# Experts of a mixture layer: picking the rows of two pairs with one set of 256-column products

## The reference, cut to what matters

```python
N_GROUPS, EXPERTS_PER_GROUP, N_EXPERTS, TOP_K, D_EXPERT = 4, 8, 32, 2, 512
# router: one group by softmax, then the two best of its eight experts, with gates
# every token goes through its two experts:
(jax.nn.silu(xb @ w1[e]) * (xb @ w3[e])) @ w2[e]      # w1, w3: 1024 x 512, w2: 512 x 1024
# results weighted by the gates are added up per token
x = x + gate2 * y_moe
return _rmsnorm(x, final_norm_w)
```

## Time and profile before

| what | us |
|---|---|
| median of 3 runs (1502.05 to 1504.66) | 1503.75 |
| the profiled execution | 1503.93 |
| its span, from first to last instruction | 1502.1 |
| mean granted TensorE clock | 0.977 |
| expert stage in the trace | about 243 to 707 |

### The profile page before, as it was taken

The page is one execution under the profiler, slowest core; times in us unless marked ns, Lnnn a source line. Parts: engine busy times, 40 slices in busy tenths (PEclk is TensorE's granted clock), DMA queues, the critical chain, the costliest instruction groups (busy, mean ns, idle before and its releaser), DMA issues.

```text
span 1502.1 us, 16975 instructions
## 1 busy us (share of the span) xinstructions
PE 1378.2 (92%) x6322; PEld 720.0 (48%) x6322; DVE 789.1 (53%) x1912; ACT 292.8 (19%) x714; POOL 340.8 (23%) x321
## 2 busy tenths in 40 slices
PE   6999999999999999999999999997997787778787
PEld 4886665444444444443566665553543332323333
DVE  2257665322332332333426887757676766767555
ACT  1435312000000000001334333221212121212112
POOL 0005303000000000000000345444544443444451
PEclk9999999999999999999999999999999999998899
DMA  9743788999999999999342699999999999999997
GB/s 381 299 158 130 282 329 309 426 426 425 426 425 426 427 426 427 425 426 425 146 175 106 267 391 396 421 421 421 421 421 421 421 422 421 422 421 422 420 422 306
DMA packets 64579, 551.35 MB, mean 367 GB/s; under 512 B 9168, under 2 KB 9440, under 8 KB 11760
## 3 DMA queue, kind: packets, MB, share of 16 engines
q1 hardware_dynamic: 26080, 278.06, 44.8%
q0 software_dynamic: 38416, 272.17, 44.0%
HBM read 549.16 MB, written 1.05 MB: 366 GB/s over the span
## 4 chain that ended last, share of the span: by engine, by line
PE 63%; DMA 31%; issue 2%; ACT 1%; DVE 1%; POOL 1%; SPq 0%; POOLq 0%; DVEq 0%
DMA ring<-peer_uv_d,work 19%; PE ps L2086 13%; PE ps L1986 11%; PE ps L2138 7%; PE ps L1327 6%; DMA work<-peer_uv_d,work 4%; PE ps L1814 4%; PE ps L1321 4%; PE ps L1775 3%; PE ps L2096 3%; DMA ring<-w_ada_d 2%; PE ps L1643 2%; DMA ring<-expert_w_d 2%; DMA work<-expert_w_d 2%; DMA consts_sb<-peer_uv_d,work 2%
## 5 line engine op out<-in xcount | busy, mean ns | idle before, releaser
L1986 PE MATMUL ps<-ring,work 128*128 128x512 f32 x686 | 338.9, 636 | 78.0 <-ACT work L1258 77.1
L3355 DVE CUSTOM_DVE_ANT_0 ring<-ring,work 128x1024 f32<-128x1024 f32 x172 | 211.4, 1230 | 137.8 <-DMA ring<-peer_uv_d,work 136.1
L1986 PEld LDWEIGHTS ps<-ring,work 128*128 128x128 f32 x686 | 134.2, 202 | 260.0 <-issue 151.6
L2314 POOL DMA_INDIRECT ring<-peer_uv_d,work x170 | 187.3, 1102 | 240.6 <-PE ps L1986 215.6
L2086 PE MATMUL ps<-ring,work 128*64 128x512 f32 x768 | 168.1, 593 | 1.4 <-DMA ring<-expert_w_d 0.9
L1258 ACT ACTIVATE work<-consts_sb,work 128x128 f32<-128x128 f32 x256 | 85.3, 392 | 285.1 <-DVE work L3364 277.2
L2086 PEld LDWEIGHTS ps<-ring,work 128*64 128x64 f32 x768 | 56.6, 137 | 109.7 <-issue 109.7
L1327 PE MATMUL ps<-ring,hT 128*128 128x512 f32 (+1 forms) x256 | 105.7, 567 | 0.1
L2896 DVE TENSOR_TENSOR work<-work,ps 128x512 f32<-128x512 f32 x16 | 11.0, 687 | 177.2 <-PE ps L2086 177.2
L2288 POOL DMA_DIRECT2D mod<-subkeys_d x1 | 0.5, 548 | 456.3 <-DVEq L2963 456.3
L1106 ACT ACTIVATE work<-ps 128x512 f32<-128x512 f32 x16 | 9.6, 597 | 430.7 <-PE ps L2086 430.7
(11 more groups left out here) (486 smaller groups left out, 1748.3 us busy)
## 6 DMA issues: line engine op xcount, KB each, us to landing
ring<-expert_w_d SPq DMA_DIRECT2D x72, 2048.0 KB, 19.3
work<-expert_w_d SPq DMA_DIRECT2D x36, 1024.0 KB, 18.7
ring<-w_ada_d SPq DMA_DIRECT2D x12, 2048.0 KB, 9.3
ring<-w_in_d SPq DMA_DIRECT2D x11, 2048.0 KB, 22.7
consts_sb<-expert_w_d SPq DMA_DIRECT2D x12, 1024.0 KB, 19.7
ring<-w_out_d SPq DMA_DIRECT2D x4, 2048.0 KB, 8.3
ring<-peer_w_query_d SPq DMA_DIRECT2D x4, 2048.0 KB, 7.9
ring<-w_in_d SPq DMA_DIRECT2D x4, 1024.0 KB, 30.0
```

Source lines behind the costliest of these rows:

```text
L1986: last = pe.matmul(ps[V_BANK[t] + n][:, :], diag[:, i % 4, :], v_row(i)[:, n * 512:(n + 1) * 512], start=(i % (16 * PH) == 0), stop=(i == ...
L2314: pool.indirect_dma_start(out=uv_rows(i), out_offset=None, in_=io["peer_uv"], in_offset=bass.IndirectOffsetOnAxis(ap=idx[:, s, k:k + 1], a ...
L3355: dve.tensor_tensor_reduce(out=u_row(i), in0=u_row(i), in1=h_tok[:, i // (16 * PH), :], scale=1.0, scalar=0.0, op0=ALU.mult, op1=ALU.add, ...
```

## The change

Pair 0 and pair 15 are still picked alone; the pairs 1 and 2, 3 and 4, ..., 13 and 14 are picked together (`gathered_with`), by 16 products of 256 columns in four banks, during the even pair ahead of them. The tiles pm and xeT hold two pairs and have moved, with pg and pgT, to other addresses. An odd pair picks nothing: between its layer "b" and the transposes it spreads two of the four results of the pair before, the other two come after the transposes, and its w3 tiles are given free by the first transpose. VectorE follows the same order; it makes the masks of two pairs in an even pair. The number of places stays eight; place and turn of a tile are worked out by two functions with the same values as before. GpSimd zeroes qz after the experts instead of before (its old address is now pm's). The waits for the two biases become one semaphore, so that the first waits for both. The dense branch has other addresses for its tiles.

```diff
@@ -254,16 +254,34 @@
         return self.turn[i - self.banks] if i >= self.banks else None
+def gathered_with(p):
+    return 2 if 0 < p < PAIRS - 1 else 1
+def tile_place(n):
+    return n % PLACES
+def tile_turn(n):
+    return sum(tile_place(m) == tile_place(n) for m in range(n + 1))
 def expert_jobs():
     jobs = [("g00", "D"), ("g01", "D")]
     for p in range(PAIRS - 1):
         jobs += [(f"a{p}", "A"), (f"b{p}", "D")]
-        jobs += [(f"g{p + 1}0", "D"), (f"g{p + 1}1", "D")]
-        jobs.append((f"at{p}", "D"))
-        if p:
-            jobs += [(f"sc{p - 1}{n}", "D") for n in range(4)]
+        if p % 2 == 0:
+            jobs += [(f"g{p + 1}{i}", "D") for i in range(2 * gathered_with(p + 1))]
+            jobs.append((f"at{p}", "D"))
+            jobs += [(f"sc{p - 1}{n}", "D") for n in range(4 if p else 0)]
+        else:
+            jobs += [(f"sc{p - 1}0", "D"), (f"sc{p - 1}1", "D"), (f"at{p}", "D")]
+            jobs += [(f"sc{p - 1}2", "D"), (f"sc{p - 1}3", "D")]
         jobs.append((f"pt{p}", "D"))
...
@@ -474,17 +492,18 @@
         acc = W(2048, TT, D)
-        xeT = W(4096, KC, P)
-        pm = W(5120, TT, P)
-        pg = W(5376, 2, TT, P)
-        pgT = W(5888, TT, P)
+        xeT = W(4096, KC, 2 * P).rearrange("p k (j n) -> p k j n", j=2)
+        pm = W(11776, TT, 2 * P)
+        pg = W(12288, 2 * TT, P).rearrange("p (j t) n -> p j t n", j=2)
+        pgT = W(12800, TT, P)
         sil = W(6144, D_EXP)
         act_p = W(6656, D_EXP)
         actT = W(7168, 4, P)
         y_sb = W(9984, D)
         sil_d = W(4096, 4, T)
         act_d = W(6144, 4, T)
-        acc_s = mod[:, 1:3, :]
+        acc_s = W(0, TT, D)
+        hT_d = [W(5120, 4, T), mod[:, 2, :].rearrange("p (k n) -> p k n", k=4)]
         beside = [[W(2048, 2048), W(13312, 2048)], [consts[:, C_LINC:C_LINC + 2048], W(7680, 2048)]]
...
@@ -1766,14 +1785,16 @@
             def gathered(p):
-                pe.wait_ge(p_ready, p + 1)
-                for g in range(2):
+                pairs = gathered_with(p)
+                width, per = pairs * P, 4 // pairs
+                pe.wait_ge(p_ready, p + pairs)
+                for g in range(2 * pairs):
                     b = fbank(f"g{p}{g}")
-                    for c in range(4):
-                        k = 4 * g + c
+                    for c in range(per):
+                        k = per * g + c
                         for t in range(TT):
-                            last = pe.matmul(b[:, c * P:(c + 1) * P], h_tok[:, t, k * P:(k + 1) * P],
-                                             pm[:, t, :], start=(t == 0), stop=(t == TT - 1))
+                            last = pe.matmul(b[:, c * width:(c + 1) * width], h_tok[:, t, k * P:(k + 1) * P],
+                                             pm[:, t, 0:width], start=(t == 0), stop=(t == TT - 1))
                             if p and k == 0 and t == 0:
...
@@ -2079,11 +2100,13 @@
                     wt = [expert_tile(p, l + u) for u in range(2)]
+                    j = (p - 1) % 2 if gathered_with(p) == 2 else 0
+                    per = 4 // gathered_with(p)
                     for k in range(KC):
-                        if k % 4 == 0:
-                            taken(f"g{p}{k // 4}")
+                        if k % per == 0:
+                            taken(f"g{p - j}{k // per}")
                         for u in range(2):
-                            last = pe.matmul(b[u * CAP:(u + 1) * CAP, :], xeT[:, k, u * CAP:(u + 1) * CAP], wt[u](k),
+                            last = pe.matmul(b[u * CAP:(u + 1) * CAP, :], xeT[:, k, j, u * CAP:(u + 1) * CAP], wt[u](k),
                                              start=(k == 0), stop=(k == KC - 1), skip_group_check=True)
...
@@ -2112,22 +2135,23 @@
                     first_layer(p, "b", 2)
-                    if p < PAIRS - 1:
+                    if p % 2 == 0:
                         gathered(p + 1)
+                    elif p < PAIRS - 1:
+                        scattered(p - 1, 0)
+                        scattered(p - 1, 1)
                     else:
                         scattered(p - 1, 2)
                     b = fbank(f"at{p}")
                     taken(f"b{p}")
                     for c in range(4):
                         last = pe.transpose(b[:, c * P:(c + 1) * P], act_p[:, c * P:(c + 1) * P], ident)
-                        if c == 0 and p == PAIRS - 1:
+                        if c == 0 and p % 2:
                             last.then_inc(w_used, 2)
                     last.then_inc(f_done, 1)
                     if p:
-                        for i in range(4 if p < PAIRS - 1 else 0):
+                        for i in (3,) if p == PAIRS - 1 else (2, 3) if p % 2 else range(4):
                             scattered(p - 1, i)
-                        if p == PAIRS - 1:
-                            scattered(p - 1, 3)
                     turned_places(p)
...
@@ -2276,8 +2303,6 @@
             pool.dma_start(k_nw, io["moba_k_norm_w"].to_broadcast([P, AD])).then_inc(b2_small, 16)
-            for t in range(TT):
-                pool.memset(qz[t], 0.0).then_inc(qz_zero, 1)
             pool.wait_ge(nw_used, 1)
...
@@ -2287,6 +2312,8 @@
             pool.dma_start(mod[:, 0, :], io["norm2_w"].to_broadcast([P, D])).then_inc(in_nw3, 16)
+            for t in range(TT):
+                pool.memset(qz[t], 0.0).then_inc(qz_zero, 1)
             pool.wait_ge(nw_used, 2)
...
@@ -2548,7 +2575,7 @@
                 post(na_sc)
-            dve.wait_ge(in_bias, 16)
+            dve.wait_ge(in_bias_mod, 32)
             window_scores(0)
...
@@ -2818,7 +2845,8 @@
                         e = 2 * p + u
-                        dve.tensor_scalar(pm[:, t, u * CAP:(u + 1) * CAP], io64, rk[:, t, e:e + 1], None,
+                        at = (p - 1) % 2 * P * (gathered_with(p) - 1) + u * CAP
+                        dve.tensor_scalar(pm[:, t, at:at + CAP], io64, rk[:, t, e:e + 1], None,
                                           ALU.is_equal).then_inc(sel_n, 1)
...
@@ -2870,9 +2898,12 @@
                 def rows_in(p):
-                    for g in range(2):
+                    pairs = gathered_with(p)
+                    per = 4 // pairs
+                    for g in range(2 * pairs):
                         b = fjob(f"g{p}{g}")
-                        ftook(dve.tensor_copy(xeT[:, 4 * g:4 * g + 4, :], b[:, :].rearrange("p (c n) -> p c n", c=4)))
+                        ftook(dve.tensor_copy(xeT[:, per * g:per * (g + 1), 0:pairs, :],
+                                              b[:, :].rearrange("p (c j n) -> p c j n", c=per, j=pairs)))
                 def added(p, pieces=range(4)):
...
@@ -2887,21 +2918,24 @@
                     if p < PAIRS - 1:
-                        places(p + 1)
+                        for later in range(p + 1, p + 1 + gathered_with(p + 1)) if p % 2 == 0 else ():
+                            places(later)
                         weighted_places(p + 1)
                     else:
                         added(p - 1, (0, 1))
                     b = fjob(f"b{p}")
                     dve.wait_ge(f_a, FAST.taken(f"a{p}"))
                     ftook(dve.tensor_tensor(act_p, sil, b[:, :], ALU.mult))
-                    if p < PAIRS - 1:
+                    if p % 2 == 0:
                         rows_in(p + 1)
+                    elif p < PAIRS - 1:
+                        added(p - 1, (0, 1))
                     else:
                         added(p - 1, (2,))
                     b = fjob(f"at{p}")
                     ftook(dve.tensor_copy(actT.rearrange("p a b -> p (a b)"), b[:, :]))
                     if p:
-                        added(p - 1, range(4) if p < PAIRS - 1 else (3,))
+                        added(p - 1, (3,) if p == PAIRS - 1 else (2, 3) if p % 2 else range(4))
                     b = fjob(f"pt{p}")
...
```

More of the change, by code:

```diff
@@ L864, in _ @@
                 for q in range(24):
+                    n = PLACES + q
                     sp.wait_ge(w_used, i * 24 + (q + 3))
-                    expert_tile(i * 8 + (2 * ((8 + q) // 6) + q % 2), (8 + q) % 6, q % PLACES)
-            for q in range(72, N_MOE - PLACES):
-                sp.wait_ge(w_used, q + 3)
-                expert_tile(2 * ((8 + q) // 6) + q % 2, (8 + q) % 6, q % PLACES)
+                    expert_tile(i * 8 + (2 * (n // 6) + n % 2), n % 6, q % PLACES)
+            for n in range(PLACES + 72, N_MOE):
+                sp.wait_ge(w_used, n - PLACES + 3)
+                expert_tile(2 * (n // 6) + n % 2, n % 6, tile_place(n))
             for i in range(len(tiles2)):
@@ L1759, in expert_tile @@
             def expert_tile(p, l):
-                place, turn = (6 * p + l) % PLACES, (6 * p + l) // PLACES + 1
+                place, turn = tile_place(6 * p + l), tile_turn(6 * p + l)
                 if place < RING:
@@ L2166, in _, with full_pairs, tile_of @@
                 pe.wait_ge(full_copied, 2 * TT)
-                with pe.Fori(0, PAIRS // 4) as i:
```

(29 more changed lines are left out.)

17 lines of the change are left out of this document (8 added, 9 removed).

## The result

| kernel | median us (runs) | profiled execution, span |
|---|---|---|
| before | 1503.38 (22) | 1503.93, 1502.1 |
| after | 1506.20 (22; 1504.65 to 1508.25) | 1507.81, 1505.9 |

The ratio is 1.0018 [1.0012, 1.0024]: 2.7 us (1.8 to 3.6) slower, where 1.8 us was forecast. The range held it. One run of before, 1536.02 us, was in a slower state and is left out of the ratio. The profiled execution of after is one of its slower ones, so I read stages in it, not its total.

What follows compares the result with a forecast made beforehand. The prediction took the weight-tile transfers to bound the expert stage, with TensorE arriving at the same moment. From the profiled 1503.93 us (median 1503.75), +1.8 for one hole and 0 for the rest gave 1505.6 us, range 1501.0 to 1508.0.

Steps and rivals of the forecast that it cites:

- What bounds the stage: Expert stage: it ends when the weight-tile transfers end, 29.5 us a pair against 28.61 us of TensorE.
- The saving: Picking on TensorE: 0.35 us less for each of seven couples, 2.45 us in all, worth nothing by itself.
- The late release at pair 1: Pair 1's first products, which free pair 0's output tiles, come 3.33 us later, from 273.91 to 277.2.
- The size of the hole: Gap in the tile transfers near 278 us: 3.33 - 1.5 = 1.8 us, bounds 0.8 and 2.8.
- the slack of 1.5 us: The tile issue at 275.1 could come as late as 276.6 without breaking the stream of transfers.
- the bound of 2.8: Upper bound in us of the gap, if the landing at 279.6 was late through one DMA engine of 16.
- the rival without slack: At the issue of 275.1 the whole 3.33 us slip is lost, 1507.1 us; chance 0.18 together with two holes.
- The page's fixed part: About 2.0 us fixed per DMA by the skill page, against 2.9 from the rows; gives a 0.9 us hole.
- Later places: Tile issues after the first gap, in pair 1 and at pair 3 (slack 1.2 to 2.2 us): no second gap.
- TensorE's waits: Waits for expert tiles grow from 2 us to some 6; waits of 1 to 2 us leave the clock at 1.00.
- The end: End of the expert stage: last tile landing and TensorE's arrival each 1.8 us later, last landing near 697.2.
- Small edits: Merged bias wait, moved memsets, final-norm weights fetched 1 us earlier: worth nothing, covered by idle time or the natural hole.

Runs made afterwards that it cites:

- twice_pair8: The kernel before the change with the picking of pair 8's rows done twice, in pair 7; 1504.54 us, ratio 1.0005.
- twice_pair1: The kernel before the change with the picking of pair 1's rows done twice, in pair 0; 1506.31 us, ratio 1.0020.
- pick_after_output: The changed kernel with pair 0's double picking put behind pair 0's output layer; 1505.84 us, ratio 1.0013 to the kernel before.
- single_start: The changed kernel with pairs 1 and 2 picked alone, couples beginning with 3 and 4; 1505.18 us, ratio 1.0007 to the kernel before.
- small_edits: The kernel before the change with only the merged bias semaphore and the later memsets; 1503.92 us, ratio 1.0005.

## Why the prediction was right, and where it was off

- **What bounds the stage: right.** The transfers do. TensorE had 1.6 us less to do and the stage grew; twice_pair8 shows the other side, 3.6 us more work for 0.9.
- **The saving: nearly.** 0.35 us for each couple was forecast, 0.23 came (57.22 - 56.99), and it was hidden. The picking itself takes the 7.01 us of the earlier trace rows; what is missing is the first two spreads of an odd pair, 1.82 us (291.86 to 293.68) where 1.72 was reckoned.
- **The late release at pair 1: right, and shown alone** by twice_pair1. Shift 3.33 us, as forecast.
- **The size of the hole: 1.8 forecast, 2.55 measured.** The step that was mis-sized is the slack of 1.5 us, read from one execution. There the tile issued at 262.8 landed at 279.6, a microsecond late; my sum leaned on that microsecond, though the bound of 2.8 named it. In after the forerunner was 0.4 us less late against the stage's start, so the lead was 0.74 and not 4.44 - 3.33 = 1.11. The restart took 8.2 us and not 7.8, another 0.4. With 1.8 these are the 2.55, so that of a shift of 3.33 only 0.8 us was covered: halfway between the forecast and the rival without slack. The slack of one execution was taken for that of all; 4.44 and 4.00 us of lead at the same issue in before and twice_pair8 show how it moves.
- **The page's fixed part: it didn't decide.** The 2.0 us that the prediction quotes from the Trainium skill ("DMA: Bandwidth & Descriptors", Anatomy of one DMA) stand there for transfers that GpSimd issues; these are SyncE's. The restarts here leave 2.9 to 3.7 us beyond the tile, and the hole of 0.9 us by the page did not come.
- **Later places: right for after, and only because of the hole.** At pair 3 the lead is 342.3 - 336.2 = 6.1 us. Without the hole it is 2.8 in pick_after_output, where stalls of TensorE in pair 0 delay pair 3 by 1.1 us on top, and 3.3 in single_start: about the edge. I had counted the hole into that slack and hadn't asked what the place would be like without it.
- **TensorE's waits: right in sum, wrong in form.** Six microseconds were forecast. By the pairs' distances 6.7 went (4.46 + 0.19 + 2.07 over an unstalled pair), where before lost 2.6; 4.4 of them are waits and some 1.7 the half clock. "Waits of 1 to 2 us did not lower it" said more than the earlier trace rows shows, a single wait of 1.07; and the surplus of two pairs comes as one wait.
- **The end: right in kind, and the number by luck.** Last landing 697.6 for 697.2, but 0.8 us of that is the later start of the stage. Within the stage the last landing came 1.3 us later and TensorE's arrival 2.4, where I had 1.8 for both. Both fell together in before because a tile there landed 1.1 us late at 675.7, behind TensorE's last wait; in after no tile does, and TensorE comes 1.2 us behind the last landing. The end hangs on the landing that pair 14 waits for, not on the last one.
- **VectorE: right.** Its copies of the turned activations, in pair 0 and in pair 1, and the stall of 0.72 us ahead of 271.11:

```profile
269.77 0.69 DVE L2905 COPY work<-ps 128x512 f32<-128x512 f32 x1 [1.03 <-PE ps L1796]
270.38 0.68 DVE L2936 COPY work<-ps 128x512 f32<-128x512 f32 x1
...
294.49 0.68 DVE L2936 COPY work<-ps 128x512 f32<-128x512 f32 x1
```

  The second ends at 295.17, 1.0 us before the output layer of pair 1 begins (0.9 forecast).
- **Small edits: right**, by the starts of the stage in all traces and by GpSimd's own row: the memsets stand ahead of 23.27 us of idle time.

```profile
713.04 1.02 POOL L2316 MEMSET work<- 128x512 f32 x2
737.34 0.53 POOL L2318 DMA_DIRECT2D nw<-mix_scale_d  x1 [23.27 <-DVEq L3260]
```

**What stays open.** The 2.3 to 2.6 us of pick_after_output are only in part accounted for: its stage is 1.3 to 1.4 us longer and its stream 1.1 to 1.2, of which the two thin places are 0.2 to 0.5. Why the tile issued at 293.1 and 295.2 is a microsecond late both times isn't shown. Landings that are 0.5 to 1.9 us late occur in every execution, before too, at changing places, and make the stage differ by about a microsecond. Which executions lose time to the clock can't be read from their times alone.

## What to carry to other kernels

Where a bounded number of buffers feeds a stream of transfers, look at each early release by its lead, the time from its issue to its forerunner's landing, and ask for each what remains when work is moved ahead of it; take the latest harmless issue from how long a restart takes on a dry queue, and don't count on a late landing of one execution. Read an engine's busy time over the stage that the change touches: over the whole span it fell by 3.8 us here, none of it in that stage. A saving on the engine that isn't the slower one turns into waiting; if the edit also bunches the waits, the clock can take as much as the edit gave (1.7 against 1.6 us here). When one thin place is mended, the next one of the same kind has to be read again, since the hole had been its cover.

## What the runs showed that I had not expected

The profiled execution of small_edits was 3.5 us longer than the median, and its stage was not. On VectorE one operation of 128x256, begun at 119.66, took 4.74 us instead of 0.4 (5.04 us for two, before 0.71). GpSimd had begun a 128x2048 operation 0.23 us earlier, and the two end 0.3 us apart. At 140.75 it happened again, with an operation of 4.63 us begun 0.03 us behind GpSimd's next one. First VectorE and GpSimd in small_edits, then in before:

```profile
119.36 5.04 DVE L2508 TENSOR_TENSOR ring<-ring,consts_sb 128x256 f32<-128x256 f32 x2
...
119.43 7.19 POOL L2227 TENSOR_TENSOR ring<-ring 128x2048 f32<-128x2048 f32 x2 [2.21 <-ACT ring L1001]
...
140.48 4.90 DVE L2556 TENSOR_SCALAR work<-work,small 128x256 f32<-128x256 f32 x2
140.72 4.51 POOL L2227 TENSOR_TENSOR ring<-ring 128x2048 f32<-128x2048 f32 x1 [7.14 <-ACT ring L1001]
```
```profile
119.70 0.71 DVE L2509 TENSOR_TENSOR ring<-ring,consts_sb 128x256 f32<-128x256 f32 x2
...
120.27 6.99 POOL L2228 TENSOR_TENSOR ring<-ring 128x2048 f32<-128x2048 f32 x2 [2.72 <-ACT ring L1002]
```

In before GpSimd begins 0.14 us before VectorE's pair of operations ends, and nothing is held. So it is in the twelve other traces: the second of VectorE's pair begins 0.06 to 0.68 us ahead of GpSimd's operation (in twice_pair8 0.01 us behind it) and takes 0.41 us. What counts seems to be whether GpSimd is already under way. The stage of small_edits then started 3.9 us later than that of before (251.77 against 247.89). Some runs of before itself, 1506.9 to 1509.3 us where its median is 1503.6, may be the same race won the other way; none of them has a trace. In this one execution the meeting of two engines cost more than the change does.
